# Dense experts of a first layer: each down product two tiles behind its up product instead of one

## The reference, cut to what matters

```
q = (h @ w_query).reshape(..., 8 heads, 2, 64);  s = q . sub_keys
s_top, i_top = top_k(s, 16);  cand = all 16 x 16 sums;  best, pos = top_k(cand, 16)
eid  = chosen expert numbers;  gate = softmax(best)
act  = gelu(einsum('chkd,cd->chk', u_tab[eid], h)) * gate
out  = einsum('chk,chkd->cd', act, v_tab[eid])
```

## Time and profile before

| | |
|---|---|
| median of 3 runs | 4086.73 us (4082.15 to 4087.82) |
| profiled execution | 4085.21 us, span 4083.4 us |
| TensorE matmul busy | 3591.4 us (88%) |
| VectorE busy | 2362.9 us (58%) |
| GpSimd busy | 889.4 us (22%) |
| ScalarE busy | 649.1 us (16%) |
| DMA | 1096.67 MB, mean 269 GB/s |
| up products L1667 | 2048 records, 380 ns mean, 464.9 us |
| down products L1676 | 2048 records, 391 ns mean, 485.1 us, 81.8 us idle before them |

### The profile page before, as it was taken

One profiled execution on the slowest core, in us unless ns is written; L12 is line 12 of the kernel. 1 busy time (PEld: TensorE's weight loads), 2 busy tenths in 40 slices (PEclk: granted clock), 3 DMA queues, 4 the chain that ended last, 5 costly groups with the idle time before them and its releaser, 6 DMA issues. The chain is left out here.

```text
span 4083.4 us, 41719 instructions
## 1 busy us (share of the span) xinstructions
PE 3591.4 (88%) x14914; PEld 2631.6 (64%) x14914; DVE 2362.9 (58%) x4846; ACT 649.1 (16%) x1760; POOL 889.4 (22%) x776
## 2 busy tenths in 40 slices
PE   7989987798888999988997776655999999999999
PEld 3678875687777777776784322222777676777676
DVE  2654778977788767776548887776352401352400
ACT  2531111400000000005212111101001301001300
POOL 0000000165565555540004444442000000000000
PEclk9999997999999999999999888776999999999999
DMA  4466545799999999982668999997883345683343
GB/s 173 152 178 195 148 140 204 233 392 409 409 408 369 409 409 409 408 339 90 175 186 337 417 421 383 423 422 318 277 300 112 134 155 166 222 306 114 134 155 113
DMA packets 523735, 1096.67 MB, mean 269 GB/s; under 512 B 25844, under 2 KB 339188, under 8 KB 489494
## 3 DMA queue, kind: packets, MB, share of 16 engines
q1 hardware_dynamic: 408824, 554.12, 40.0%
q0 software_dynamic: 110592, 536.92, 32.6%
q10 hardware_dynamic: 4128, 3.15, 0.3%
HBM read 1078.36 MB, written 15.73 MB: 268 GB/s over the span
## 5 line engine op out<-in xcount | busy, mean ns | idle before, releaser
L2556 PE MATMUL ps<-hT,wring 128*128 128x256 f32 x2560 | 559.7, 379 | 1.7 <-DMA wring<-in_ffn_w_up 1.7
L1676 PE MATMUL ps<-hT,wring 128*128 128x256 f32 x2048 | 485.1, 391 | 81.8 <-DVE hT L1836 79.3
L2556 PEld LDWEIGHTS ps<-hT,wring 128*128 128x128 f32 x2560 | 485.8, 190 | 85.3 <-issue 13.1
L1676 PEld LDWEIGHTS ps<-hT,wring 128*128 128x128 f32 x2048 | 388.4, 194 | 174.0 <-DVE hT L1836 120.3
L1710 POOL DMA_INDIRECT gu<-in_u_tab,eid x256 | 285.5, 1115 | 948.1 <-POOLq L134 621.4
L1667 PE MATMUL ps<-hT,wring 128*128 128x256 f32 x2048 | 464.9, 380 | 1.1 <-ACT G L1749 1.1
L1667 PEld LDWEIGHTS ps<-hT,wring 128*128 128x128 f32 x2048 | 390.5, 191 | 54.5 <-issue 1.1
L2032 PE MATMUL ps<-pairs,diag 128*128 128x512 f32 x520 | 290.2, 719 | 134.0 <-ACT diag L2127 134.0
L1860 DVE SCALAR_TENSOR_TENSOR wring<-gv,wgt,wring 128x1024 f32<-128x1024 f32 x254 | 326.6, 1286 | 109.1 <-DMA gv<-in_v_tab,eid 97.2
L1843 DVE CUSTOM_DVE_ANT_0 gu<-gu,htok 128x1024 f32<-128x1024 f32 x256 | 313.2, 1224 | 121.8 <-DMA gu<-in_u_tab,eid 116.2
L1716 POOL DMA_INDIRECT gv<-in_v_tab,eid x256 | 290.6, 1135 | 220.3 <-DVE wring L1860 154.7
(11 more groups left out here) (385 smaller groups left out, 4561.8 us busy)
## 6 DMA issues: line engine op xcount, KB each, us to landing
wring<-in_u_first SPq DMA_DIRECT2D x128, 512.0 KB
wring<-in_v_tab SPq DMA_DIRECT2D x128, 512.0 KB
room<-in_ada_w SPq DMA_DIRECT2D x32, 1536.0 KB, 11.5
wring<-in_ffn_w_gate SPq DMA_DIRECT2D x44, 1024.0 KB, 8.9
wring<-in_ffn_w_up SPq DMA_DIRECT2D x44, 1024.0 KB, 11.4
wring<-in_ffn_w_down SPq DMA_DIRECT2D x44, 1024.0 KB, 5.0
wring<-in_w_in SPq DMA_DIRECT2D x72, 512.0 KB, 6.6
wring<-in_w_mod SPq DMA_DIRECT2D x28, 1024.0 KB, 5.6
```

The costliest lines, as they stand in the source:

```text
L1676: m = nc.tensor.matmul(ps[:, n // 2, (n % 2) * S:(n % 2 + 1) * S], vslot[:, e % 2, n * P:(n + 1) * P], act_[:, e % 3, :], start=e == 0 and ...
L2556: m = mm(ps[:, b + n, q * S:(q + 1) * S], up_slot(s, q)[:, k, n * P:(n + 1) * P], hT[:, k, 0:S], start=k == 0, stop=k == KD - 1)
```

## The change

down(e) moves from behind up(e+1) to behind up(e+2); two down products are left behind the last up product. `act_` gets a fourth place in `hT`, and gelu_all(e) waits for down(e-4) instead of down(e-3). On SP every load_v moves one round later, so that it is released by the same down product and stands in front of the same release. turn_acc(0) and turn_acc(1) keep their rounds of the loop; since down is a tile later in it, they now stand behind down(62) and down(125).

```diff
-        act_, ids, keyrow = hT[:, 0:3, 0:S], self.ids, self.rstd[:, 0:NKEY]
+        act_, ids, keyrow = hT[:, 0:4, 0:S], self.ids, self.rstd[:, 0:NKEY]
...
-                for e in range(NE):
-                    load_v(e)
+                for e in range(NE + 1):
+                    if e:
+                        load_v(e - 1)
                     if e + 2 < NE:
                         load_u(e + 2)
                     q, part = (e - 1) // FIRSTS - 1, (e - 1) % FIRSTS
...
-                        m = nc.tensor.matmul(ps[:, n // 2, (n % 2) * S:(n % 2 + 1) * S], vslot[:, e % 2, n * P:(n + 1) * P], act_[:, e % 3, :],
+                        m = nc.tensor.matmul(ps[:, n // 2, (n % 2) * S:(n % 2 + 1) * S], vslot[:, e % 2, n * P:(n + 1) * P], act_[:, e % 4, :],
...
                 for e in range(NE):
                     up(e)
-                    if e:
-                        down(e - 1)
+                    if e >= 2:
+                        down(e - 2)
                     if e - 1 == turn_after:
                         turn_acc(0)
                     if e == NE - 1:
                         turn_acc(1)
+                down(NE - 2)
                 down(NE - 1)
...
                     act.wait_ge(dfull.sem, e + 1)
-                    if e >= 3:
-                        act.wait_ge(vdone.sem, e - 2)
-                    nc.scalar.activation(act_[:, e % 3, :], ps[:, 4 + e % 2, 0:S], ACT.Gelu_apprx_tanh).then_inc(active.sem, 1)
+                    if e >= 4:
+                        act.wait_ge(vdone.sem, e - 3)
+                    nc.scalar.activation(act_[:, e % 4, :], ps[:, 4 + e % 2, 0:S], ACT.Gelu_apprx_tanh).then_inc(active.sem, 1)
...
-                    x = act_[:, e % 3, :].rearrange("p (b t) -> p b t", t=TB)
+                    x = act_[:, e % 4, :].rearrange("p (b t) -> p b t", t=TB)
```

## The result

Changed kernel: median 4089.72 us over 19 runs (4085.47 to 4093.3), against 4083.53 us (4077.65 to 4088.82) for the kernel before in the same sessions. The ratio is 1.0014 (95% interval 1.0008 to 1.0021), that is 5.7 us slower (3.3 to 8.6). The forecast was 6.4 us slower. The change's loss is real, but smaller than the 0.2% that was called the bound to no change.

The account below looks back on a forecast made before the run. The prediction took the DMA engines at 408 GB/s to bound the stage. Steady part 0, start -0.5, middle +0.5 and end +6.4 summed to +6.4 us: 4091.6 on the profiled execution, 4093 for the median, range 4083 to 4100.

Parts of the forecast that it names:

- The end: End of the stage: two down products instead of one behind the last transposition, at a lower clock; +6.4 us, bounds +3.45 to +10.5.
- The steady part: The 955 us of dense tiles: TensorE still stops for weighing, DMA engines set the pace; cost 0, 79.3 us of waits stay.
- rival 1: TensorE is the bound and its 79.3 us stall goes, giving 4007 us; chance 3%.
- Rival 2: 408 GB/s is no DMA ceiling; more requests in the air raise it to 423, giving 4059 us; chance 4%.
- ScalarE's new wait: Steady part: the wait for the down product of e - 3, claimed done before the up product ScalarE awaits anyway; cost 0.
- the signs that were named for being right: Among them, over 830 to 1815 us: rate again 408 GB/s, TensorE's waits for weighing still tens of us.
- The start: First tiles: up(2) before down(0) reaches VectorE about 3.5 us sooner; taken as -0.5 us, bounds 0 and -3.2.
- The middle: First transposition, now behind down(62): SP issues no dense load from 1329 to 1347 us; +0.5 us, bounds 0 and +3.9.
- a sign of being wrong: Around the middle transposition: a hole in the DMA rate would show the prediction wrong.
- Rival 4: Slower: the middle transposition starves the DMA engines, 3.9 us more, giving 4097 us; chance 17%.
- rival 3: Holes in the DMA rate (30 us at 279 GB/s, and the start) fill: 4087 us half filled, 4080 all; chance 18%.

Follow-up runs that it names:

- Experiment 1: Changed kernel with only the last transposition of acc put back behind down(126), leaving one down product behind it; ratio 0.9998 (0.9989 to 1.0007) to the kernel before.
- Experiment 2: Kernel before with only the last transposition moved in front of down(126), leaving two down products behind it; ratio 1.0016 (1.0007 to 1.0025) to the kernel before.
- Experiment 3: Changed kernel with 16 useless matmuls keeping TensorE busy before the last transposition's wait; end 8.11 us in the trace, ratio 1.0005 (0.9996 to 1.0014) to the kernel before.
- Experiment 6: Changed kernel loading only half of each dense down tile, work unchanged; 4013.56 us, ratio 0.9822 (0.9807 to 0.9837) to the kernel before.
- experiment 7: Changed kernel with 4 instead of 8 matmuls per dense down product of tiles 3 to 124, loads unchanged; ratio 1.0008 (0.9999 to 1.0018) to the kernel before.
- Experiment 5: Changed kernel with ScalarE's gelu_rows one tile later, behind the next tile's gelu_all; ratio 1.0015 (1.0006 to 1.0024) to the kernel before.
- Experiment 4: Changed kernel with the first transposition of acc put back behind down(63), end left as changed; ratio 1.0015 (1.0006 to 1.0024) to the kernel before.

## Why the prediction was right

**The end** was the term that carried the sum, and its size held: +6.33 us in the trace for +6.4, +5.7 in the runs. Experiments 1 and 2 show that it is necessary and sufficient: without it the change costs nothing that the runs can tell (0.9998), and alone it costs the old kernel as much (1.0016). Experiment 3 splits it as the sum did, 3.48 for 3.45 and 2.85 for the clock's share of 2.9.

**The steady part at 0** held, and so did the reason: the DMA engines. Experiment 6 takes bytes and gets nearly all their time back, experiment 7 takes TensorE's work and gets none. So rival 1 (4007) falls. Rival 2 (4059) fails too: over the long stretches the rate stayed at 408 and 406 GB/s, and so it did in experiment 7 with still more waiting in TensorE.

**Where it was wrong, without a price.** "It still stops: down(e) needs weighted(e)" is not what happens. TensorE stops mostly one instruction earlier, at up products, since ScalarE's gelu_all of the next tile stands behind gelu_rows, which waits for VectorE's dots. I had cost ScalarE's new wait and not looked at what its old queue holds back once TensorE is ahead. So one of the signs that were named for being right didn't come: waits for weighing of tens of us became 11.4 us. Experiment 5 gives the predicted picture back by moving that queue, with the time unchanged.

**The start** was taken at -0.5. In the changed kernel's profile up(2) waited 1.91 us for its load, and 5.24 us passed from its start to the next product's, at a low clock. So VectorE weighed tile 2 10.78 us behind tile 0 instead of 12.86, 2.1 us sooner and not 3.5. In the profiles of Experiments 1 and 4, whose start is the same, up(2) ran at full speed, and tile 2 was weighed 9.81 and 9.15 us behind tile 0, 3.1 and 3.7 us sooner. No gain in time can be told from the scatter. Rows of the changed kernel:

```profile
820.65 5.41 PE L1668 MATMUL ps<-hT,wring 128*128 128x256 f32 x16 [1.91 <-DMA wring<-in_u_first]
...
825.89 3.62 PE L1677 MATMUL ps<-hT,wring 128*128 128x256 f32 x16
...
826.58 0.43 DVE L1838 TENSOR_TENSOR hT<-hT,G 128x256 f32<-128x256 f32 x1 [1.84 <-ACT hT L1758]
```

**The middle** was taken at +0.5 between 0 and 3.9. The silence of SP came as foreseen, a little longer (issues at 1321.69 and 1342.48, 20.8 us apart, for 18). The gathers did not fill all of it: the hole is 1.7 us and not 0.5 in this profile, and a hole there had been named as a sign of being wrong. Experiment 4 finds no cost beyond its resolution, and Experiment 1 leaves at most 2.9 us. Rival 4's mechanism exists; its price isn't seen in the time. Of rival 3 next to nothing came: the 30 us stretch carried 286 GB/s for 279, 0.2 MB or half a microsecond.

That the -0.5 and the +0.5 cancel in the sum is a guess that no run tests one by one. Experiment 1 measures them together with the steady part: 0.9998, so between 4.5 us faster and 2.9 us slower.

## What to carry to other kernels

Before an engine's stall is moved, ask who waits for that engine: here hardly anybody did, and nearly 80 us of waiting went from one product to the other and back at no gain. What an offset in a pipeline surely changes is its two ends, so count what is left behind the last dependence, and at what clock it will run. An instruction that waits long belongs behind the work that is already free to run.

## What was not expected of the hardware

A wait of 2.25 us in front of the first down product left TensorE at full speed. One of 1.91 us in front of the third product of the changed kernel was followed by 5.24 us until the next product's start, and by a granted clock of 0.83 over 820 to 830 us (first line below). Experiment 1's kernel has the same start. There the same product waited longer, 2.62 us, and the next one started 3.56 us after it; the granted clock over 820 to 830 us was 1.00 (the other two lines). So the length of the last wait alone doesn't tell whether the clock falls, not even for the same product of the same code. What does tell stays open.

```profile
820.00:830.00 10.00, 9.35 (x36) 7.91 (x37) 7.88 (x17) 0.59 (x2) 5.58 (x5) 0.83 0.99 392
```
```profile
824.26 3.72 PE L1668 MATMUL ps<-hT,wring 128*128 128x256 f32 x16 [2.62 <-DMA wring<-in_u_first]
...
827.82 3.62 PE L1677 MATMUL ps<-hT,wring 128*128 128x256 f32 x16
```
